# Three norms share their normalisation between ScalarE and VectorE, a quarter of their transposes moves behind the first high products, and ga reads x whole

## The reference

```python
for layer in range(DEPTH):                       # DEPTH = 2
    mix = _even_mixer(...) if layer % 2 == 0 else _odd_mixer(...)
    x = _layer_norm(ALPHA * x + mix, ln1_g[layer], ln1_b[layer])
    x = _layer_norm(ALPHA * x + _swiglu(x, ...), ln2_g[layer], ln2_b[layer])
```

## Time and profile before

| | us |
|---|---|
| median of 3 runs (1242.52 to 1243.76) | 1242.6 |
| the profiled execution | 1242.73 |
| its span, first to last instruction | 1240.9 |
| TensorE busy in the span | 1226.9 |
| VectorE, ScalarE, GpSimd busy | 439.5, 450.8, 588.2 |
| mean granted TensorE clock | 0.997 of full speed |

### The profile page before, as it was taken

One profiled execution on the slowest core, in us unless ns is written; L12 is line 12 of the kernel. 1 busy time (PEld: TensorE's weight loads), 2 busy tenths in 40 slices (PEclk: granted clock), 3 DMA queues, 4 the chain that ended last, 5 costly groups with the idle time before them and its releaser, 6 DMA issues.

```text
span 1240.9 us, 17146 instructions
## 1 busy us (share of the span) xinstructions
PE 1226.9 (99%) x7108; PEld 1011.8 (82%) x7108; DVE 439.5 (35%) x772; ACT 450.8 (36%) x670; POOL 588.2 (47%) x280
## 2 busy tenths in 40 slices
PE   9999999999999999999999999999999999999997
PEld 7877887888888888887777888888788888888885
DVE  5556526201011100127779845654511011110105
ACT  4167825222223221215544455542532223221211
POOL 4243444943444343445744347444684444435341
PEclk9999999999999999999999999999999999999998
DMA  9322052333332333332243333124233322324221
GB/s 319 98 69 69 7 164 69 102 102 102 102 94 78 104 124 112 102 102 63 90 125 114 97 109 94 27 69 137 68 102 102 95 91 86 102 85 147 75 102 68
DMA packets 106065, 122.96 MB, mean 99 GB/s; under 512 B 18947, under 2 KB 80581, under 8 KB 105989
## 3 DMA queue, kind: packets, MB, share of 16 engines
q1 hardware_dynamic: 98244, 118.56, 29.9%
q10 hardware_dynamic: 7744, 3.32, 1.1%
HBM read 117.93 MB, written 3.70 MB: 98 GB/s over the span
## 4 chain that ended last, share of the span: by engine, by line
PE 93%; DVE 4%; ACT 1%; POOL 1%; DVEq 0%; ACTq 0%; issue 0%
PE bank L1666 26%; PE bank L1667 26%; PE bank L1668 26%; PE bank L2098 4%; PE bank L1697 1%; PE bank L1698 1%; PE bank L1710 1%; DVE stats L1240 1%; DVE x_tm L1238 1%; PE bank L1929 1%; PE bank L2207 1%; POOL w_lo L681 1%; PE bank L1732 1%; PE bank L2044 1%; PE bank L2190 0%; PE bank L1856 0%
## 5 line engine op out<-in xcount | busy, mean ns | idle before, releaser
L681 POOL TENSOR_TENSOR w_lo<-w_raw,w_hi 128x1024 fp32r<-128x1024 f32 (+1 forms) x200 | 470.6, 2375 | 545.8 <-ACT w_hi L816 520.9
L1666 PE MATMUL bank<-x_hi,w_hi 128*128 128x512 f32 x880 | 344.3, 391 | 0.0
L1667 PE MATMUL bank<-x_lo,w_hi 128*128 128x512 f32 x880 | 342.5, 389 | 0.0
L1668 PE MATMUL bank<-x_hi,w_lo 128*128 128x512 f32 x880 | 342.5, 389 | 0.0
L816 ACT ACTIVATE w_hi<-w_raw 128x1024 fp32r<-128x1024 f32 (+1 forms) x200 | 196.3, 1032 | 205.7 <-issue 160.4
L1666 PEld LDWEIGHTS bank<-x_hi,w_hi 128*128 128x128 f32 x880 | 165.1, 188 | 35.5 <-issue 0.8
L1668 PEld LDWEIGHTS bank<-x_hi,w_lo 128*128 128x128 f32 x880 | 165.2, 188 | 34.1
L1667 PEld LDWEIGHTS bank<-x_lo,w_hi 128*128 128x128 f32 x880 | 165.2, 188 | 33.9
L1247 DVE TENSOR_TENSOR f_ab<-bank,f_ab 128x512 f32<-128x512 f32 x44 | 30.4, 692 | 364.8 <-PE bank L1668 364.8
L1668 PE MATMUL bank<-w_hi,h_lo 128*128 128x512 f32 x352 | 136.9, 389 | 0.0
L1666 PE MATMUL bank<-w_hi,h_hi 128*128 128x512 f32 x352 | 136.9, 389 | 0.0
(11 more groups left out here) (297 smaller groups left out, 1257.9 us busy)
## 6 DMA issues: line engine op xcount, KB each, us to landing
w_raw<-ffn_w_gate_dram SPq DMA_DIRECT2D x22, 1024.0 KB, 5.3
w_raw<-ffn_w_up_dram SPq DMA_DIRECT2D x22, 1024.0 KB, 5.3
w_raw<-ffn_w_down_dram SPq DMA_DIRECT2D x20, 1024.0 KB, 5.0
w_raw<-od_w_in_dram SPq DMA_DIRECT2D x16, 1024.0 KB, 5.8
w_raw<-ev_w_in_dram SPq DMA_DIRECT2D x8, 1024.0 KB, 6.0
w_raw<-ev_w_out_dram SPq DMA_DIRECT2D x4, 1024.0 KB, 5.0
w_raw<-od_w_out_dram SPq DMA_DIRECT2D x4, 1024.0 KB, 5.4
x_fm<-x_fm_dram SPq DMA_DIRECT2D x8, 256.0 KB, 6.7
```

What stands on the lines that cost most here:

```text
L681: pool.tensor_tensor(w_lo[:, b % 2, c], w_raw[:, b % 2, c], w_hi[:, b % 2, c].bitcast(F32), ALU.subtract).then_inc(w_lo_ready, 1)
L1666: pe.matmul(out_ap, st[0], mv_[0], start=start, stop=False)
L1667: pe.matmul(out_ap, st[0], mv_[1], start=False, stop=False)
L1668: return pe.matmul(out_ap, st[1], mv_[0], start=False, stop=stop)
```

## The change

- `fm_block` with `fresh` goes feature by feature over both output tiles; after feature 2's high products it turns features 6 and 7 of all four token tiles (8 transposes). `turn_x` ahead of it turns features 0 to 5 (24). The units and banks follow; a swap in the ring is gone.
- In norms 1 to 3 ScalarE normalises tiles 0 to 2, as x * (1 / deviation) + nm_rstd, and counts halves in the new semaphore `z_act`; VectorE makes the reciprocal and nm_rstd = -mean / deviation right after each aggregate, and normalises tile 3 only, counted in `z_norm`. GpSimd waits for that tile's two halves.
- ScalarE splits the first piece of block b + 1 between `layer_norm` and `round_x` and the second after `round_x`. In norm 2 the loads of ba_w and the two constants come after that.
- ga uses x_fm, unsplit, in one pass of eight features in place of two. x_tm's load waits for ga and stands behind gv's second block in SyncE's queue.
- ScalarE splits gr's second block ahead of the copies of gv tiles 2 and 3.
- Norm 4: the product with gamma comes ahead of the wait for the square root; the reciprocal follows it.

```diff
...
+NOW = 6
 EVEN_FILLERS = [[("gr", t)] for t in range(NT)]
...
-    def ln(i):
-        u.extend(("xT", i, k) for k in range(KD))
+    def ln(i, features=range(NOW)):
+        u.extend(("xT", i, k) for k in features)
...
         for f in range(0, KF, 2):
-            u.extend([("gate", layer, f), ("gate", layer, f + 1), ("up", layer, f), ("up", layer, f + 1)])
+            u.extend([("gate", layer, f), ("gate", layer, f + 1)])
+            if f == 0:
+                ln(2 * layer + 1, range(NOW, KD))
+            u.extend([("up", layer, f), ("up", layer, f + 1)])
         for half in range(2):
...
         if i == 1:
+            ln(2, range(NOW, KD))
             u.append(("ba_fm",))
...
             turn += 1
-        if key[0] == "xT" and key[2] == KD - 1:
-            a = turn % len(ring)
-            c = (turn + 1) % len(ring)
-            ring[a], ring[c] = ring[c], ring[a]
         order[b] = len(slots)
...
         rstd = sb("rstd", [P, NT])
+        nm_rstd = sb("nm_rstd", [P, NT])
         TH = NT * GDN_H
...
             at = [2]
-            load_until(first_block[("gk",)])
+            load_until(first_block[("gr",)])
             low_part_there(sp, 0, KD - 2)
             low_part_there(sp, 0, KD - 1)
+            full(sp, ("ga",))
             sp.dma_start(x_tm[:, :, :], A["x"][0].rearrange("(t p) d -> p t d", p=P)).then_inc(s["x_landed"], 16)
...
                 if b in turned:
-                    pool.wait_ge(s["z_norm"], 2 * NT * turned[b])
+                    pool.wait_ge(s["z_norm"], 2 * turned[b])
                     split_lo(b + 1, (0,))
...
-            def round_x(i):
+            def split_part(b, j):
+
+                assert split[0] == b
+                if j == 0:
+                    act.wait_ge(w_landed[b % 2], 16 * (b // 2 + b % 2))
+                    act.wait_ge(*block_end[b - 2])
+                    low_weights_all(act, b - 2)
+                act.activation(w_hi[:, b % 2, pieces(b)[j]], w_raw[:, b % 2, pieces(b)[j]], ACT.Copy).then_inc(w_hi_ready, 1)
+                split[0] += j
+
+            def round_x(i, b):
...
                                             bias=bias), ("xT", i, k))
+                split_part(b, 1)
-            def layer_norm(i):
+            def layer_norm(i, b=None):
                 for t in range(NT):
...
                        .then_inc(s["ln_stat"], 1)
+                    if i < 4 and t < NT - 1:
+                        act.wait_ge(s["nm_ready"], (NT - 1) * (i - 1) + t + 1)
+                        for h in range(2):
+                            cols = x_tm[:, t, h * 512:(h + 1) * 512]
+                            act.activation(cols, cols, ACT.Identity, scale=rstd[:, t:t + 1], bias=nm_rstd[:, t:t + 1])\
+                               .then_inc(s["z_act"], 1)
+                if b is not None:
+                    split_part(b, 0)
...
             for t in range(NT):
+                if t == 2:
+                    split_to(first_block[("gr",)] + 1)
                 full(act, ("gv", t))
                 take(act.activation(g_v[:, t, :], bank(("gv", t))[:, :], ACT.Copy), ("gv", t))
-            split_to(first_block[("gr",)] + 1)
...
             split_to(first_block[("gate", 0, 0)])
-            layer_norm(1)
-            split_to(first_block[("gate", 0, 0)] + 1)
-            round_x(1)
+            layer_norm(1, first_block[("gate", 0, 0)] + 1)
+            round_x(1, first_block[("gate", 0, 0)] + 1)
...
             split_to(first_block[("conv", KD)])
-            layer_norm(2)
-            split_to(first_block[("conv", KD)] + 1)
+            layer_norm(2, first_block[("conv", KD)] + 1)
+            round_x(2, first_block[("conv", KD)] + 1)
...
                 act.dma_start(dst[:, :], A["c_odd"][:, c0:c0 + n]).then_inc(consts, 16)
-            round_x(2)
...
             split_to(first_block[("gate", 1, 0)])
-            layer_norm(3)
-            split_to(first_block[("gate", 1, 0)] + 1)
-            round_x(3)
+            layer_norm(3, first_block[("gate", 1, 0)] + 1)
+            round_x(3, first_block[("gate", 1, 0)] + 1)
             ffn(1)
...
                 def normalise(t):
-                    dve.wait_ge(s["ln_stat"], NT * (i - 1) + t + 1)
-                    link(dve.reciprocal(rstd[:, t:t + 1], rstd[:, t:t + 1]))
                     if i == 4:
...
                         dve.wait_ge(s["ln_landed"], 32 * 4)
+                        dve.wait_ge(s["ln_var"], NT * (i - 1) + t + 1)
                         for h in range(2):
...
                                                      ALU.subtract, ALU.mult).then_inc(y_ready[t], 1)
+                        dve.wait_ge(s["ln_stat"], NT * (i - 1) + t + 1)
+                        link(dve.reciprocal(rstd[:, t:t + 1], rstd[:, t:t + 1]))
                         for h in range(2):
...
                         return
+                    dve.wait_ge(s["ln_stat"], NT * (i - 1) + t + 1)
+                    link(dve.reciprocal(rstd[:, t:t + 1], rstd[:, t:t + 1]))
                     for h in range(2):
...
                                .then_inc(s["ln_var"], 1)
-                            if i == 4:
+                            if i == 4 or t == NT - 1:
                                 normalise(t)
-                            elif t:
-                                normalise(t - 1)
-                if i < 4:
-                    normalise(NT - 1)
+                            else:
+                                dve.wait_ge(s["ln_stat"], NT * (i - 1) + t + 1)
+                                link(dve.reciprocal(rstd[:, t:t + 1], rstd[:, t:t + 1]))
+                                dve.scalar_tensor_tensor(nm_rstd[:, t:t + 1], mv[:, t, 0:1], -1.0, rstd[:, t:t + 1],
+                                                         ALU.mult, ALU.mult).then_inc(s["nm_ready"], 1)
...
                     for n in range(len(keys)):
-                        if k == 0:
-                            high(0, n)
-                            high(1, n)
-                        elif k > 1:
-                            high(k, n)
+                        high(k, n)
+                    if k == 2:
+                        turn_x(fresh, range(NOW, KD))
                     for kl in [k - 2] * (k > 1) + [KD - 2, KD - 1] * (k == KD - 1):
...
-            def few_columns(key, w):
+            def few_columns(key, w, parts):
...
                 quarters = P // SB
-                for j, x in enumerate((x_hi, x_lo)):
+                for j, x in enumerate(parts):
                     for k in range(KD):
...
                         ins = pe.matmul(ps[q * SB:(q + 1) * SB, :], w[:, k, :], x[:, k, :].bitcast(F32),
-                                        start=j == 0 and k < quarters, stop=j == 1 and k >= KD - quarters,
+                                        start=j == 0 and k < quarters, stop=x is parts[-1] and k >= KD - quarters,
                                         skip_group_check=True)
...
-            def turn_x(i):
+            def turn_x(i, features=range(NOW)):
                 for t in range(NT):
-                    for k in range(KD):
-                        if k % 4 == 0:
-                            pe.wait_ge(s["z_norm"], 2 * (NT * (i - 1) + t) + k // 4 + 1)
+                    for k in features:
+                        if k % 4 == 0 and t < NT - 1:
+                            pe.wait_ge(s["z_act"], 2 * ((NT - 1) * (i - 1) + t) + k // 4 + 1)
+                        elif k % 4 == 0:
+                            pe.wait_ge(s["z_norm"], 2 * (i - 1) + k // 4 + 1)
                         ps = fill(("xT", i, k)) if t == 0 else bank(("xT", i, k))
...
             fm_block(first_block[("gk",)], [("gk", 0), ("gk", 1)])
-            few_columns(("ga",), ga_w)
+            few_columns(("ga",), ga_w, (x_fm,))
             for t in range(NT):
...
                     pe.wait_ge(s["ba_landed"], 16)
-                    few_columns(("ba_fm",), ba_w)
+                    few_columns(("ba_fm",), ba_w, (x_hi, x_lo))
                 if i == 2:
```

More of the change, by code:

```diff
@@ L530, in trunk_kernel @@
         s = {n: sem(n) for n in (
-            "eye_landed", "x_landed", "ln_landed", "warm_ready", "w_first_hi", "w_first_lo", "x_hi_ready", "x_lo_even", "x_lo_odd", "z_norm", "half_stats", "ln_stat", "ln_var",
+            "eye_landed", "x_landed", "ln_landed", "warm_ready", "w_first_hi", "w_first_lo", "x_hi_ready", "x_lo_even", "x_lo_odd", "z_norm", "z_act", "nm_ready", "half_stats", "ln_stat", "ln_var",
             "x_affine", "out_sent", "act_step", "dve_step", "o_hi_ready", "h_hi_ready", "h_lo_ready",
```

## The result

The changed kernel takes **1248.37 us** (median of 5 runs, 1247.71 to 1248.43) against 1242.6 before (5 runs, 1242.52 to 1243.76): ratio 1.0041, 95% interval 1.003 to 1.0052. I had forecast 1240.3 and a range of 1238.7 to 1242.1. The profiled execution took 1248.37 as well, 5.64 more than before; its span is 1246.6. It is slower by more than twice what a measurement can tell, and by none of the mechanisms that I had priced.

A forecast was written before the change was run, and what follows sets the result against it. TensorE, busy nearly the whole span, was taken as the bound, with VectorE bounding the end. Terms -1.3 (final norm), -0.7 (norms 1 to 3) and -0.3 (ga) sum to -2.3: median 1240.3 us, range 1238.7 to 1242.1.

The forecast's parts named there:

- rival (c): Norms 1 to 3: eight moved transposes cost their duration, 2.2 us, giving 1244.1; chance 0.06 together with a table-reload rival.
- Final norm, -1.3: Norm 4: subtraction and gamma product ahead of the square root's wait save 0.33 us per tile, four times.
- Start of the projections, -0.91: Norms 1 to 3, hand-over to TensorE: the projection's first product comes 0.91 us earlier per norm (-0.18 - 0.61 - 0.12).
- Order of the products, -0.26: Projections after norms 1 to 3: four products on feature 0 first take back 0.26 of 0.37 us lost.
- eight moved transposes, +0.95: Norms 1 to 3: transposes moved from idle time into the product stream cost 0.95 us per norm, bounds 0.87 to 1.5.
- Norms together, -0.7: Norms 1 to 3: hand-over, product order and moved transposes sum to -0.22 us per norm, -0.7 for three.
- ga, -0.3: ga to gr 0: one pass saves 1.78 us, but ScalarE holds leave only 0.3 us of gain.
- first brake: ScalarE splits weights until 64.2, so the copies of ga and qT 2 come 1.04 us earlier; TensorE's shift is 1.05.
- second brake: Second gr block's split ahead of the copies of gv 2 and gv 3 holds gr 0 until 93.5.
- rival (a): ga's gain comes through, 1.5 us more, with gr's low weights 1.8 earlier: 1238.8 us; chance 0.14.
- Hidden parts: ScalarE's extra halves, the put-off weight piece and the loads of ba_w and x: taken to cost nothing.
- The spacing of products: TensorE's products: taken to follow one another every 0.2275 us, so 48 take 10.92 us.

The follow-up runs named there:

- b_pad32: Kernel before with 32 unused bytes ahead of the buffers behind rstd, so h_hi and h_lo begin 32 bytes later: 1249.49 us, ratio 1.005.
- c_same: Changed kernel whole, but with nm_rstd in the 16 unused bytes behind rstd, so no other buffer changes its address: 1241.64 us, ratio 0.9989.
- b_final_norm: Kernel before with only the reciprocal of the final norm's tiles moved behind the two gamma operations: 1241.85 us.
- c_unmoved: c_same with all eight features of each norm turned ahead of the projection, old order of banks and first products: 1239.71 us.
- b_ga_final: Kernel before with ga in one pass, x_tm's load behind it, and the final norm's reciprocal moved: 1240.43 us, ratio 0.9979.

## Why the prediction was wrong

**The failed step is the costing of `nm_rstd`.** The prediction priced its instruction ("The small new VectorE product (minus mean over deviation) is like the reciprocal, 0.15, and lies in the wait for the next tile") and not its buffer: the sum -1.3 - 0.7 - 0.3 has no term for addresses, which puts it at nothing without a reason. I listed the banks, queues, engines and DMAs that each edit touches, and not the addresses that a new allocation moves. That term is +6.6 us (b_pad32; 6.7 between c_same and the change): 1056 products of the `down` stages go every 0.2333 us and not every 0.2267. It turned a gain of 1.3 into a loss of 5.8. No rival covered it either: rival (c), the one on the slower side, had to be false, and was. The chance of 0.04 for slower was the chance of the mechanisms that I had seen.

The rest, by its own steps:

- *Final norm, -1.3.* Right in mechanism, about a fifth too large: the adds are 4.80 apart, not 4.73, so 0.26 a tile, 1.07 in all by the table and 0.91 in b_final_norm. After's chain:

```profile
1224.98 0.70 DVE x_tm L1262
1225.70 0.70 DVE stats L1264
...
1226.76 0.81 DVE x_tm L1220 x2
...
1228.28 0.75 DVE x_tm L1227
...
1229.79 0.70 DVE x_tm L1262
```

The pair now starts 1.78 us after the add's start and not 2.22, 0.44 earlier where I had 0.52; and from there to the next add it is 3.03 and not 2.84 (5.06 less 2.22), the 0.19 that I had. So the first figure was off: I took 0.03 between aggregate and pair, and it is 0.1.

- *Start of the projections, -0.91.* Right: the first product of norm 2 stands 4.39 us behind the old products in c_same and not 5.27, so -0.88. The normalisation of tile 3 follows its add by 2.22 and not 2.83 us, the 0.61 that I had; the first product follows that by 1.85 and not 2.05, 0.20 where I had 0.12. The add itself gained 0.07 and not 0.18: in c_same VectorE still trails a little behind TensorE, because the new product was mis-sized. The first of a norm is no 0.15 in c_same's timeline of VectorE, and GpSimd's timeline shows what is different about it:

```profile
552.09 1.03 DVE L1250 SCALAR_TENSOR_TENSOR rstd<-mv,rstd 128x1 f32<-128x1 f32 x1
...
555.43 0.16 DVE L1250 SCALAR_TENSOR_TENSOR rstd<-mv,rstd 128x1 f32<-128x1 f32 x1
```

```profile
548.34 4.76 POOL L684 TENSOR_TENSOR w_lo<-w_raw,w_hi 128x1024 fp32r<-128x1024 f32 x2 [6.12 <-ACT w_hi L819]
```

GpSimd is in a subtraction that ends at 553.10, and the product ends at 553.12; at 555.43 GpSimd is idle.

- *Order of the products, -0.26, and eight moved transposes, +0.95.* Together +0.69; c_same has 12.07 us from the first product to the block's end and before 11.28, +0.79. Each within its bounds. The eight take 0.87, and the 36 products behind them 8.19 (566.11 to 574.30), where before they took 8.15 (565.98 to 574.13): 0.91, near the lower bound. So rival (c) fell: a transpose lasts 279 ns here, but one starts every 0.11 us also amid products. About 275 ns is also what the Trainium skill gives on its page "TensorE: Matmul & The Clock Gate", section "Part 4: PE-mode transpose". It was the order of the products that gave less than the 0.26 I took: the first twelve take 3.01 (562.23 to 565.24) and took 3.13, 0.12 less.

- *Norms together, -0.7.* Measured -0.19, -0.20 and -0.11 by the table, -0.5; norm 2 gives only -0.09 in c_same (16.46 after 16.55), where TensorE is not slowed ahead of it. I had computed that the moved transposes cost more than the new order returns, and didn't draw the conclusion that the part is better left out; c_unmoved shows it.

- *ga, -0.3.* Measured -0.43 with the mechanism as forecast. TensorE in the changed kernel:

```profile
94.31 0.50 PE L1690 MATMUL bank<-w_hi,x_hi 128*128 128x512 f32 x1 [1.41 <-ACT g_v L957]
```

gr 0 starts at 94.31, or 93.47 on before's scale without the 0.84 of the start; I had 93.5. The first brake was sized right too, 1.04 let through in b_ga_final for 1.05. Without the second brake the old wait for GpSimd's low weights goes as well, as rival (a) had argued from their coming 1.8 earlier, and b_ga_final gains 1.8. So rival (a) would have been right for the old place of the split.

- *Hidden parts.* ScalarE's six halves a norm, the put-off weight piece, the load of ba_w and the moved load of x cost nothing that the trace shows, as forecast: none of TensorE's waits is for them, and no table load stands between a norm's roots and the passes behind them. The one table load of a norm comes ahead of its first root, before and after. The Trainium skill's page "ScalarE: Activation LUTs", section "Rules for kernel authors", advises VectorE for such arithmetic. Here a half takes 0.76 us on ScalarE and 0.5 on VectorE, and yet the slower engine is the better place, with the put-off piece by 0.67 us a norm: it was idle, and VectorE was on the chain.

- *The spacing of products.* The prediction and several expectations go by 0.2275 us; the stages have 0.2267. For 48 products that is 10.88 and not 10.92, so that 0.40 us and not 0.37 were lost in norm 2, and 1056 products at 0.2333 cost 7.0 and not 6.1 to 6.5.

Without the shifted addresses the forecast would have been 1.3 too low against c_same (1241.64), inside its range, with a gain of 1.3 where 2.3 was forecast.

## What to carry to other kernels

Read the allocations in a diff, too. A small buffer put ahead of large ones moves them all, and on this kernel 32 bytes cost 2.9% on each product (0.2333 us for 0.2267) of the groups whose two operands were no longer a multiple of 256 bytes apart. Where a group of untouched instructions changes its mean duration, compare the addresses before anything else, and where a change is tested, put its new buffers last or into slack, so that it is the change that is timed.

And price each half of a combined edit by itself: here the order of a split took back most of the pass that ga saved, and two moved features took back most of what ScalarE gave.

## What the runs showed of the hardware

- fp32 products of 128x128 by 128x512 with both operands in SBUF go every 0.2267 us when stationary and moving buffer are a multiple of 256 bytes apart, every 0.2333 when they are 32 or 64 bytes off it, and every 0.2324 at 128 bytes. Shown with h as the stationary operand, and with x in either place (shifted by 32 only). That it is the distance and not the address rests on one run with the base shifted by 32 bytes; that it is the distance between the two operands, and not to another buffer, was not tested apart. Why it is so was not tested; nor was 256 told apart from distances between 128 and 256, or the rounding of the rows inside the buffers, which are multiples of 512 bytes here.
- The first `nm_rstd` product on VectorE of each norm took 0.94 to 1.03 us, the later ones 0.16. In the six traces that have it, all 18 slow ones run beside a subtraction (L684 in c_same) on GpSimd and end within 0.02 us of its end; none of the 36 fast ones has GpSimd at work beside it. It is not the operation's first use: the add 2.2 us earlier is a SCALAR_TENSOR_TENSOR as well. So the product seems to be held until GpSimd is done; no run moved either of them to prove it.
- Runs of one kernel spread over 1.3 us (1242.46 to 1243.79 in 65 runs). One difference was seen at the very start, 4.36 to 5.49 us for twelve warm-up products, which sets the start of all that follows. The spread is as wide as the largest term of the sum in the prediction, so such terms are read from one chain's own stretches, as above, and not from the difference of two single runs.
